# Splitting the gate-chunk stores, spreading the first gathers and V-group loads, and moving one exponent by two tiles

## The reference

```python
def peer_ffn(h, w_q, keys, u_tab, v_tab):
    ...
    q = (ht @ w_q).reshape(t, PEER_HEADS, 2, PEER_HALF)
    sc = jnp.einsum('thid,hikd->thik', q, keys).astype(jnp.float32)
    top_s, top_i = lax.top_k(sc, PEER_TOPK)
    cand = top_s[:, :, 0, :, None] + top_s[:, :, 1, None, :]
    best_s, best_pos = lax.top_k(cand.reshape(t, PEER_HEADS, PEER_TOPK * PEER_TOPK), PEER_TOPK)
    i1 = jnp.take_along_axis(top_i[:, :, 0], best_pos // PEER_TOPK, axis=-1)
    i2 = jnp.take_along_axis(top_i[:, :, 1], best_pos % PEER_TOPK, axis=-1)
    experts = i1 * N_KEYS + i2
    gates = jax.nn.softmax(best_s, axis=-1).astype(h.dtype)
    ...
    def block(args):
        hb, eb, gb = args
        act = jnp.einsum('thkd,td->thk', u_tab[eb], hb)
        coef = gb * jax.nn.gelu(act, approximate=False)
        return jnp.einsum('thk,thkd->td', coef, v_tab[eb])
```

## Time and profile before

| | |
|---|---|
| median of three runs | 3256.0 us |
| the profiled execution | 3247.32 us, its span 3245.6 us |
| TensorE busy, matmul | 3078.6 us (95% of the span) |
| VectorE, ScalarE, GpSimd busy | 75%, 47%, 26% |
| moved by DMA | 840.83 MB, mean 259 GB/s |
| U stage of the first layer | about 476 to 1118 us of the span |
| its V stage | about 1118 to 1663 us |

### The profile page before, as it was taken

The page is one execution under the profiler, slowest core; times in us unless marked ns, Lnnn a source line. Parts: engine busy times, 40 slices in busy tenths (PEclk is TensorE's granted clock), DMA queues, the critical chain, the costliest instruction groups (busy, mean ns, idle before and its releaser), DMA issues.

```text
span 3245.6 us, 47711 instructions
## 1 busy us (share of the span) xinstructions
PE 3078.6 (95%) x17460; PEld 2859.4 (88%) x17460; DVE 2436.0 (75%) x4276; ACT 1510.6 (47%) x2394; POOL 844.4 (26%) x655
## 2 busy tenths in 40 slices
PE   6988899999999999999989789999999999999998
PEld 3755679999999999999978468899999999999998
DVE  4564689778886688888876648995888857887887
ACT  3342223467886333333343522335878843333333
POOL 1000015544443222222200000354444422222221
PEclk8989999999999999999999889999999999999999
DMA  6524445589999999999932012467999999999996
GB/s 236 182 72 155 176 168 169 177 283 369 342 338 356 338 352 347 346 348 348 347 105 72 20 65 79 122 192 229 337 335 369 338 369 327 348 347 347 350 345 219
DMA packets 256496, 840.83 MB, mean 259 GB/s; under 512 B 23280, under 2 KB 72688, under 8 KB 248304
## 3 DMA queue, kind: packets, MB, share of 16 engines
q1 hardware_dynamic: 174000, 470.28, 41.8%
q0 software_dynamic: 80640, 318.80, 26.9%
q10 hardware_dynamic: 1728, 50.33, 3.7%
HBM read 736.56 MB, written 102.76 MB: 259 GB/s over the span
## 4 chain that ended last, share of the span: by engine, by line
PE 83%; DVE 7%; DMA 5%; ACT 4%; issue 1%; POOL 0%; DVEq 0%; SPq 0%; ACTq 0%; POOLq 0%
PE bank L815 41%; PE bank L1211 32%; PE bank L1195 4%; DMA w_raw<-wst 3%; PE bank L831 2%; PE bank L869 1%; ACT w_hi L571 1%; DMA activations<-act_out 1%; PE bank L1133 1%; DMA ada_buf<-adaw 1%; DVE w_lo L1253 1%; DMA ring<-u,gidx 0%; PE bank L964 0%; PE bank L981 0%; DVE zs L1533 0%
## 5 line engine op out<-in xcount | busy, mean ns | idle before, releaser
L571 ACT ACTIVATE w_hi<-w_raw 128x1024 fp32r<-128x1024 f32 x596 | 631.3, 1059 | 999.4 <-PE bank L815 759.8
L1253 DVE TENSOR_TENSOR w_lo<-w_raw,w_hi 128x1024 fp32r<-128x1024 f32 x516 | 632.2, 1225 | 610.2 <-ACT w_hi L571 609.3
L815 PE MATMUL bank<-hH,w_hi 128*128 128x384 f32 (+1 forms) x2656 | 948.1, 357 | 31.8 <-issue 7.9
L815 PE MATMUL bank<-hL,w_hi 128*128 128x384 f32 (+1 forms) x2656 | 928.5, 350 | 0.0
L815 PE MATMUL bank<-hH,w_lo 128*128 128x384 f32 (+1 forms) x2656 | 928.4, 350 | 0.0
L1211 PE MATMUL bank<-c_hi,w_hi 128*128 128x384 f32 x2048 | 686.1, 335 | 4.4 <-ACT act_out L747 3.2
L1211 PE MATMUL bank<-c_hi,w_lo 128*128 128x384 f32 x2048 | 684.3, 334 | 0.0
L1211 PE MATMUL bank<-c_lo,w_hi 128*128 128x384 f32 x2048 | 684.3, 334 | 0.0
L815 PEld LDWEIGHTS bank<-hH,w_hi 128*128 128x128 f32 x2656 | 504.1, 190 | 83.9 <-issue 42.5
L815 PEld LDWEIGHTS bank<-hH,w_lo 128*128 128x128 f32 x2656 | 503.2, 189 | 25.2
L815 PEld LDWEIGHTS bank<-hL,w_hi 128*128 128x128 f32 x2656 | 503.9, 190 | 22.1
(11 more groups left out here) (259 smaller groups left out, 2723.6 us busy)
## 6 DMA issues: line engine op xcount, KB each, us to landing
w_raw<-wst SPq DMA_DIRECT2D x596, 512.0 KB, 5.8
activations<-act_out SPq DMA_DIRECT2D x128, 384.0 KB, 6.5
gate_matrices<-stage ACTq DMA_DIRECT2D x12, 4096.0 KB, 17.1
act_in<-activations SPq DMA_DIRECT2D x64, 768.0 KB, 7.1
gates<-gate_matrices SPq DMA_DIRECT2D x64, 768.0 KB, 11.1
ada_buf<-adaw POOLq DMA_DIRECT2D x32, 1024.0 KB, 6.7
nrm<-adaw POOLq DMA_DIRECT2D x8, 1024.0 KB, 5.1
pj<-adaw POOLq DMA_DIRECT2D x4, 1024.0 KB, 5.5
```

The source lines that it names most:

```text
L571: nc.scalar.activation(w_hi[g % 2][:, :, :].rearrange("p a b -> p (a b)"), w_raw[:, g % RAWS, :], ACT.Copy).then_inc(s_wh, 1)
L815: last = mm(bank[s][:, 0:t.stop - t.start], a[s][:, k, :], b[:, k, t], start=(k == 0 and a is w_hi and b is hH), stop=(k == KT - 1 and a i ...
L1253: v.tensor_tensor(w_lo[g % 2][:, :, :].rearrange("p a b -> p (a b)"), w_raw[:, g % RAWS, :], w_hi[g % 2][:, :, :].rearrange("p a b -> p (a ...
```

## The change

It has four parts.
- The store of a gate chunk (4 MB, 32 KB in each partition) becomes four stores of 1 MB (8 KB in each partition, 32 keys each): one in the tile in which the chunk is full, and one in each of the three tiles after. The counts of the semaphores `s_gst` grow fourfold.
- `load_group` is cut in two, `load_acts` and `load_gates`. The first two groups are loaded ahead of the loads of tiles 116 (activations 0), 118 (gates 0), 120 (activations 1) and 122 (gates 1). The wait for all stores of the layer moves from 118 to 116. The later groups are loaded as before.
- The first five gathers are issued one behind each low part of tiles 20 to 24 instead of all behind that of tile 20.
- The first group's exponent is taken in tile 6 instead of tile 4; those of the other groups stay.

```diff
+STORES = 4
+STORE_KEYS = N_KEYS // STORES
+
+def stores_of(n):
+    return [(c, part) for c in range(GCHUNKS) for part in range(STORES)
+            if (c + 1) * CHUNK_QUADS - 1 in quads_of(n - part)]
...
-            def load_group(l, g):
+            def load_acts(l, g):
                 s = g % 2
...
                 sp.dma_start(act_in[s][:, :, :, :], a_dram[g * 2:g * 2 + 2].rearrange("q p b t -> p q b t")
                              ).then_inc(s_ain[s], 16)
+
+            def load_gates(l, g):
+
+                s = g % 2
                 sp.dma_start(gates[s][:, :, :, :],
...
+                    if n == U0 + GATE1 + 8:
+
+                        for s in range(2):
+                            sp.wait_ge(s_gst[s], (l + 1) * (GCHUNKS // 2) * STORES * 16)
+                        load_acts(l, 0)
                     if n == U0 + GATE1 + 10:
-
-                        for s in range(2):
-                            sp.wait_ge(s_gst[s], (l + 1) * (GCHUNKS // 2) * 16)
-                        load_group(l, 0)
-                    if n == U0 + GATE1 + 16:
-                        load_group(l, 1)
+                        load_gates(l, 0)
+                    if n == U0 + GATE1 + 12:
+                        load_acts(l, 1)
+                    if n == U0 + GATE1 + 14:
+                        load_gates(l, 1)
...
                         pool.wait_ge(s_gidx, l + 1)
-                        for k in range(RING):
-                            gather(l, k)
+                    if 0 <= n - (U0 + 2 * PICK_TILES) < RING:
+                        gather(l, n - (U0 + 2 * PICK_TILES))
...
-                    if tt < NT and m == 4:
+                    if tt < NT and m == (6 if tt == 0 else 4):
                         act.wait_ge(s_shift, l * NT + tt + 1)
...
-                        if i == CHUNK_QUADS - 1:
-
-                            act.wait_ge(s_gv, l * QUADS + q + 3)
-                            act.dma_start(g_dram[c].rearrange("p e t -> p (e t)"),
-                                          stage[c % 2][:, :, :].rearrange("p e t -> p (e t)")).then_inc(s_gst[c % 2], 16)
+                    for c, part in stores_of(n):
+                        e = slice(part * STORE_KEYS, (part + 1) * STORE_KEYS)
+                        act.wait_ge(s_gv, l * QUADS + (c + 1) * CHUNK_QUADS + 2)
+                        act.dma_start(g_dram[c][:, e, :].rearrange("p e t -> p (e t)"),
+                                      stage[c % 2][:, e, :].rearrange("p e t -> p (e t)")).then_inc(s_gst[c % 2], 16)
```

More of the change, by code:

```diff
@@ L91 @@
 assert [q for n in range(N_KEYS) for q in quads_of(n)] == list(range(QUADS))
+STORES = 4
[3 more added lines that the diff above has]
+            if (c + 1) * CHUNK_QUADS - 1 in quads_of(n - part)]
+assert sum(len(stores_of(n)) for n in range(N_KEYS)) == GCHUNKS * STORES
 RING = 5
@@ L464, in _ @@
                         sp.dma_start(keys[:, :, :], keysT[l]).then_inc(s_keys, 16)
+                    if n == U0 + GATE1 + 8:
+                        for s in range(2):
+                            sp.wait_ge(s_gst[s], (l + 1) * (GCHUNKS // 2) * STORES * 16)
+                        load_acts(l, 0)
                     if n == U0 + GATE1 + 10:
-                        for s in range(2):
-                            sp.wait_ge(s_gst[s], (l + 1) * (GCHUNKS // 2) * 16)
-                        load_group(l, 0)
-                    if n == U0 + GATE1 + 16:
-                        load_group(l, 1)
+                        load_gates(l, 0)
[3 more added lines that the diff above has]
+                        load_gates(l, 1)
                     if EV0 + 6 <= n < STREAM - 2 and (n - EV0 + 2) % GROUP == 0:
-                        load_group(l, (n - EV0 + 2) // GROUP)
+                        load_acts(l, (n - EV0 + 2) // GROUP)
+                        load_gates(l, (n - EV0 + 2) // GROUP)
                     load_w(l, n)
@@ L765, in _ @@
                         if i == 0 and l * GCHUNKS + c >= 2:
-                            act.wait_ge(s_gst[c % 2], (l * (GCHUNKS // 2) + c // 2) * 16)
+                            act.wait_ge(s_gst[c % 2], (l * (GCHUNKS // 2) + c // 2) * STORES * 16)
                         act.wait_ge(s_gm, l * QUADS + q + 1)
```

## The result

The changed kernel took 3203.9 us in the median of four runs (3202.3 to 3206.8), against 3253.9 of the kernel before: a ratio of 0.9841, 95% interval 0.9807 to 0.9874, 50 us or 1.6% faster. Forecast were 3223 us, 33 us faster, in a range from 3204 to 3243. The profiled execution took 3206.8 us with a span of 3205.0, against 3247.3 and 3245.6: 40.6 us less by the spans.

A forecast was written before the change was run, and what follows sets the result against it. Bound: TensorE matmul, 83% of the chain, with time to gain where it stands still or runs at lower clock. Terms -12.3 - 11 - 14 + 4 = -33.3 us took 3247.3 to 3214, plus 8.7 gave 3223; range 3204 to 3243.

The forecast's parts named there:

- Exponent, -12.3: First exponent, tile 4 of both layers: moved to tile 6, ScalarE no longer waits for VectorE's `bestv`; gain 12.3 us.
- Gathers, -11: First five gathers, GpSimd behind tile 20: spread one per tile, they no longer delay the low parts; gain 11 us.
- Middle stores, -14: Ten gate-chunk stores before each layer's last: 8 KB pieces let weight loads through; 17.1 us lost, 3 left, gain 14.
- parts that land in 5 to 8 us: Sign for the chunk stores: each 1 MB part lands 5 to 8 us after its issue.
- weight loads under 13 us: Sign for the chunk stores: weight loads take under 13 us.
- Last chunk and V groups, +4: SP's wait at tile 116 and packed V groups: 12 us lost in both layers against 7.9; cost 4 us.
- From the profile to the median, +8.7: Whole kernel: 8.7 us added to 3214, as the median shown stood that far above the profiled execution.
- (2): Chunk stores: stalls are a matter of bytes, not pieces, and stay; gain 19 us, time 3237; chance 0.17.
- (3): Tile 116: SP's wait and packed V groups cost 12 us a layer, not 6; time 3235 to 3243; chance 0.10.
- (4): All three stalls go, the last store's too: gain 48 us, time 3208; chance 0.17.
- (5): Spread gathers are late by 0.4 us in each tile: gain 29 us, time 3227; chance 0.03.
- (6): Chunk stores: four transfers hold the engines longer than one, up to 116 us for twelve, time 3349; chance 0.03.

The follow-up runs named there:

- before, again: The kernel before, unchanged, run and profiled once more: 3250.5 us in the median of eight.
- the part alone: The kernel before with only the first exponent moved from tile 4 to tile 6: 3242.7 us, ratio 0.9954.
- the split stores alone: The kernel before with only the chunk stores in four parts over four tiles: 3224.5 us, ratio 0.9910.

## Why the stores cost: the size of a piece, or how many at once

The changed kernel alters two things about a store, its pieces (8 KB for 32 KB) and its spreading over four tiles. Four kernels take them apart.

**All at once, in pieces of 8 KB.**

```diff
     return [(c, part) for c in range(GCHUNKS) for part in range(STORES)
-            if (c + 1) * CHUNK_QUADS - 1 in quads_of(n - part)]
+            if (c + 1) * CHUNK_QUADS - 1 in quads_of(n)]
```

> The changed kernel with all four parts of a chunk stored in the tile in which it is full: 4 MB at once, but in pieces of 8 KB. Theory A (turns piece by piece, size of the piece decides): a weight load beside them takes 7 to 12 us instead of 15, the four parts need about 20 us, middle stores lose 0 to 3 us in all, time within 5 us of the changed kernel. Theory B (spreading over four tiles is what helps): weight loads of 15 us and 17 us or more lost, 20 us slower than the changed kernel.

3237.2 us, ratio 0.9961 (0.9946 to 0.9975), and 38.9 us lost up to the copy behind tile 107, more than with one store of 4 MB. (4.2 of it belong to the last chunk's issues in tile 107 and are made up by the next copy, so 34.7 are the middle stores'.) The time, 33 us above the changed kernel, is nearer to theory B, but the reason is neither theory's. DMA issues, 717 to 734 us (KB each, us to landing), and the timeline of ScalarE there:

```profile
gate_matrices<-stage ACTq DMA_DIRECT2D x4, 1024.0 KB, 10.2
w_raw<-wst SPq DMA_DIRECT2D x2, 512.0 KB, 7.7
```

```profile
718.52 4.42 ACTq L796 DMA_DIRECT2D gate_matrices<-stage  x4
723.00 2.44 ACT L761 ACTIVATE oneh<-oneh,idxT 128x128 f32<-128x128 f32 x8 [4.50 <-issue]
725.35 1.04 ACT L592 ACTIVATE w_hi<-w_raw 128x1024 fp32r<-128x1024 f32 x1
```

The two weight loads of this stretch took 7.7 us, and with pieces of 32 KB it was 15.1; over both layers a load beside the parts took 8.9 us in the median. So shorter pieces do shorten the loads, and between 640 and 1010 us ScalarE waited for no transfer. But four issues in a row held ScalarE for 4.4 us here (2.7 to 4.9 us over the twelve chunks), where a single one takes 0.33, and the copy `w_hi` behind them came 3 us late or more: 9.3 us after the one before. With pieces of 8 KB it is this hold that spreading takes away.

**Two stores of 2 MB, pieces of 16 KB** (`STORES = 2`).

> The changed kernel with two stores of 2 MB over two tiles, pieces of 16 KB. By turns piece by piece a weight load takes 8 x (0.62 + 0.31) + 2.5 = 10 us, and up to 15 with the store of an activation pair ahead of it, against 14.1 + 1.9 us that it has. Theory A: 0 to 4 us lost at the ten middle stores. Theory B (bytes of one burst): half of the 17 to 26 us of before.

3209.2 us, ratio 0.9876 (0.9859 to 0.9892); 6.3 us lost at the middle stores, weight loads of 12.3 us where 10 was worked out. Between nothing at 8 KB and 17 to 26 at 32 KB. Theory A said 0 to 4 and theory B half of 17 to 26, so it is neither, nearer to A.

**Spread over four tiles, but in pieces of 32 KB, 32 neighbouring partitions each.**

```diff
-                        e = slice(part * STORE_KEYS, (part + 1) * STORE_KEYS)
+                        r = slice(part * (P // STORES), (part + 1) * (P // STORES))
...
-                        act.dma_start(g_dram[c][:, e, :].rearrange("p e t -> p (e t)"),
+                        act.dma_start(g_dram[c][r, :, :].rearrange("p e t -> p (e t)"),
```

> The changed kernel with a chunk's four parts cut by partitions instead of keys: four stores of 1 MB over four tiles, in pieces of 32 KB, two on each DMA engine. Theory A: two long rounds of 1.56 us and six short ones make a weight load of 5.0 us plus 2.5 to start, as with 8 KB; nothing lost. Theory B (pieces of 32 KB hold the weights up even in small numbers): 3 us or more lost at the middle stores.

3273.1 us, ratio 1.0061 (1.0042 to 1.0079), 70 us above the changed kernel, 59.5 us lost at the middle stores and 20 at the last. That looks like theory B, but it is one more effect. The page's queue row of the stores (packets, MB, share of 16 engines), first of this kernel, then of the next one:

```profile
q10 hardware_dynamic: 2304, 50.33, 5.1%
```

```profile
q10 hardware_dynamic: 2304, 50.33, 3.7%
```

The same bytes in the same number of packets held the engines for 5.1% of the span: 0.051 x 3273.6 x 16 / 1536 data pieces = 1.74 us for one, against 1.24 in the other.

**The same, but each part takes every fourth partition** (`r = slice(part, P, STORES)`).

> As the kernel whose parts were 32 neighbouring partitions, but each part takes every fourth partition, so that it reads from all over the buffer: four stores of 1 MB over four tiles in pieces of 32 KB. Theory A (the pieces of 32 KB were slow, 1.74 us against 1.24, because 32 neighbouring partitions share few ways out of the buffer): pieces of 1.2 us, 0 to 5 us lost at the ten middle stores, time within 8 us of the changed kernel. Theory B (long pieces hold the weights up even when few are under way): 20 us or more lost, weight loads of 12 us or more, as there.

3207.6 us, ratio 0.9857 (0.9828 to 0.9886), pieces of 1.24 us and 3.1 us lost at the middle stores. By pieces and time it is theory A. But weight loads still take 11.6 us beside such parts, where the sum of rounds in the expectation of the kernel ahead of this one gave 7.5. Which partitions a part reads costs 65 us.

**All of them together.** Where a trace has the landings, the weight loads of both layers that overlap a chunk store by over 3 us can be set beside what the middle stores lost:

| kernel | piece | stores of a chunk | load beside, median and longest | lost |
|---|---|---|---|---|
| neighbouring partitions | 32 KB | four, over four tiles | 15.0 and 19.8 us | 59.5 us |
| before, again | 32 KB | one | 13.6 and 16.4 us | 21.8 us |
| before | 32 KB | one | 13.3 and 16.1 us | 17.1 us |
| two stores | 16 KB | two, over two tiles | 12.3 and 15.5 us | 6.3 us |
| every fourth partition | 32 KB | four, over four tiles | 11.6 and 14.4 us | 3.1 us |
| changed, again | 8 KB | four, over four tiles | 10.5 and 13.9 us | 0.0 us |
| at once | 8 KB | four, in one tile | 8.9 and 10.8 us | 34.7 us, by the issues |

All but the last stand in one order: the longer the longest loads, the more is lost, and nothing is lost in the one kernel where the longest stays below the 14.1 us that the forecast gave a load from its issue to its use (in the gate tiles of the changed kernel 13.6 and 14.5 us lie between them in turn). Spreading alone brings most of that (3.1 us left), the shorter pieces the rest. Bytes are not out of it: by the forecast 477 GB/s are asked for over the four tiles and 421 can be moved, and that is the likely reason why a load in the changed kernel takes 10.5 us and not 7.5. It still comes in time, so this costs nothing.

That the engines take the queues in turn, piece by piece, can be seen in the kept trace of the kernel before. The 128 pieces of the second chunk's store, 1.21 us each, begin in eight groups of sixteen, about 1.5 us apart; in the middle of the store sixteen 4 KB pieces of SP's queue begin in each such group, as many as there are engines, and up to seventeen of the gathers. The eight pieces of an engine do not go in one run.

The Trainium skill, page SBUF — State Buffer, section Door 1: The DMA port swizzle, says that a partition's DMA port is given by bits 2 to 4 and bit 6 of its number: 32 neighbours reach 8 of the 16 ports, every fourth partition reaches all. By that rule the sixteen engines have half as many ports to read through in the one kernel as in the other. The trace agrees in direction, with 1.74 against 1.24 us, a factor of 1.4.

## The last chunk

**Wait and groups as before, rest changed.** `load_acts` and `load_gates` of group 0 ahead of 118, of group 1 ahead of 124, the wait at 118:

```diff
-                    if n == U0 + GATE1 + 8:
+                    if n == U0 + GATE1 + 10:
...
                         load_acts(l, 0)
-                    if n == U0 + GATE1 + 10:
                         load_gates(l, 0)
-                    if n == U0 + GATE1 + 12:
+                    if n == U0 + GATE1 + 16:
                         load_acts(l, 1)
-                    if n == U0 + GATE1 + 14:
                         load_gates(l, 1)
```

> The changed kernel with the first two V groups loaded as in the kernel before (both halves of group 0 ahead of tile 118, of group 1 ahead of 124, the wait for all stores at 118). Theory A (the earlier wait and the packed groups are what the last chunk still costs, 2.6 us in the first layer and 8.9 in the second): 5 to 10 us faster than the changed kernel, SP waits less than 3 us for the stores. Theory B (the bytes of these tiles decide, wherever the loads stand): within 2 us of the changed kernel.

3201.0 us (3200.0 to 3204.0), 5.3 us lost at the last chunks, SP waits at most 1.3 us for the stores. By the profiles 6 us better than the first of the changed kernel; by the medians 3, by the ratios (0.9837 against 0.9841) 1 us. The place behaves as theory A has it, the time does not reach its 5 us.

**Only the wait moved back to 116, groups at 118 and 124.**

> The changed kernel with the wait for all stores ahead of tile 116 as changed, but the V groups where they were (group 0 ahead of 118, group 1 ahead of 124). Theory A (the wait holds the weight loads back, which is what the last chunk costs): 4 to 8 us lost in the second layer behind the wait, SP stands 9 to 12 us before tile 116, time as the changed kernel. Theory B (the packed groups are what costs): 5 us lost in both layers together, as with the groups and the wait where they were.

3206.6 us, ratio 0.9856 (0.9828 to 0.9883). SP stood 8.7 us ahead of tile 116 in the second layer and yet only 2.5 us were lost there; 6.2 us in the first, with 3.9 lost, 6.5 together. That is 1.2 us more than without the wait. So a wait of 6 to 9 us in SP costs little by itself; the three tiles of weights ahead of TensorE are the likely reason, but that was not tried. Neither theory holds in full: more was lost than theory B's 5 us, and not where theory A put it.

**Groups at 118, 120, 122, 124, and at 119, 121, 123, 125.**

> The changed kernel with the wait and the first activations ahead of tile 118, the gates of group 0 ahead of 120, the activations of group 1 ahead of 122 and its gates ahead of 124. The stores have landed by then, so SP doesn't wait. Theory A (the wait is what costs): 3 to 6 us lost at the last chunks of both layers together against 11.5 in the changed kernel, 3197 to 3201 us. Theory B (bytes decide): no difference to the changed kernel.

> As the kernel with the groups from 118 on, one tile later again: ahead of 119, 121, 123 and 125, tiles that have no store of an activation pair behind them. Theory A: 1 to 5 us lost at the last chunks, 3196 to 3200 us, unless VectorE then waits for group 0 at its first product, which would cost up to 3 us a layer. Theory B (bytes decide): as the changed kernel.

3200.4 us (3198.8 to 3209.1) and 4.5 us lost; 3204.1 us (3200.0 to 3206.6) and 4.3 us lost; both have the ratio 0.9847, against 0.9841 of the changed kernel. VectorE waited for no group. The two differ by 4 us in the medians and by nothing at the place: that is the rest, 3194.4 against 3200.5, of which 4.3 us are the token mixer of the second layer and 2.4 its V stage. So theory A holds at the place in both, but a difference in time to the changed kernel isn't shown by these two.

**The three together on one chip.** Since the times above overlap, the changed kernel, the groups from 118 on, and the last chunk's four parts all in tile 107 were run side by side, five rounds each:

```diff
-            if (c + 1) * CHUNK_QUADS - 1 in quads_of(n - part)]
+            if (c + 1) * CHUNK_QUADS - 1 in quads_of(n - (0 if c == GCHUNKS - 1 else part))]
```

> The changed kernel once more, beside two variants on the same chip. Theory A (SP's wait ahead of tile 116 costs by itself): again 9 to 12 us of waiting in each layer and 8 to 12 us lost at the last chunks. Theory B (the 8.9 us of the first profile were a chance of the queues, the wait being absorbed by three tiles of weights in advance): 5 us or less. Middle stores 0.0 us in both.

> The groups from 118 on, once more (wait and first activations ahead of 118, then 120, 122, 124). Theory A: 3 to 6 us faster than the changed kernel on this chip, losses at the last chunks 4 to 5 us. Theory B: within 2 us of it.

> As the kernel before this, but the last chunk of a layer is stored in its own tile, four parts of 1 MB one behind the other, the other five spread over four tiles. Where all chunks went at once, the last ones lost only 1.0 us in both layers. Theory A (the last chunk's store should be through before the V groups come, and ScalarE has the time for four issues behind tile 107): 1 to 2 us lost at the last chunks, 2 to 4 us faster than the kernel before this. Theory B (ScalarE is held 4.4 us by four issues in a row and copies late, as in the middle): 5 us or more lost.

| kernel | median, range | ratio to before | last chunk | SP's wait, two layers |
|---|---|---|---|---|
| changed | 3203.6, 3199.6 to 3209.0 | 0.9847 | 7.3 us | 10.2 and 10.6 us |
| groups from 118 on | 3200.3, 3198.1 to 3202.4 | 0.9837 | 3.9 us | 1.6 and 2.4 us |
| last chunk at once | 3200.7, 3199.0 to 3203.2 | 0.9838 | 4.6 us | none |

The second profile of the changed kernel has 7.3 us where the first had 11.5, so part of the 8.9 of the second layer was chance. Theory A of the changed kernel's repeat asked for 8 to 12 us and theory B for 5 or less, so neither is met. With the groups from 118 on, 3.4 to 7 us less is lost at the place. In time, only this last comparison was made side by side, and it gives 3.3 us, 0.1%, with intervals of 0.17% either way; the earlier ratios to before (0.9837 and 0.9847 against 0.9841) give 1 us for and 2 against. So a gain of the later groups in the whole time is not shown. Storing the last chunk at once gains nothing further, nearer to theory B than to A, but not for theory B's reason: the issues held ScalarE for 3.4 and 4.3 us, the copy behind them came 1.0 and 2.2 us late, and the next copy made up all of it. The 4.6 us lie in the tiles behind, 109 to 114, where ScalarE waited for weight loads. The 1.0 us that the expectation took from the kernel with all chunks at once was a matter of booking: with tile 107 counted in, that kernel lost 5.2 us at its last chunks.

## Why the prediction was right or wrong

**Exponent, -12.3:** right to the tenth in both layers (0 left of 12.3), and the part alone gave 0.46%. What was said to be next, the exponent of tile 14, waited 1.25 us instead of 0.3, harmless for the reason given.

**Gathers, -11:** right; 11.4 came, all of it. The 0.5 us kept back for slow gathers were not needed: they took 0.95 to 1.00 us each, not the mean of 1.41, which is as short as before (0.93 us was the shortest). Why the mean is longer was not tried.

**Middle stores, -14: the term of the sum that was mis-sized.** In the mean 21.5 us were there to be had and all of it came. The mechanism held: the queues take turns by single pieces, as the starts of the pieces show, and a load that keeps within its 14.1 us costs nothing. Two sizes were off. The 17.1 us that I took as what is lost was the least of four profiles of kernels with big stores: 17.1, 20.7, 21.8, 26.2, mean 21.5. And I left 3 us, because more bytes are asked for in those four tiles than the engines move; 0.0 us were left in every kernel with 8 KB parts over four tiles. The surplus did show, but in the loads: beside parts they took 10.4 us in the median where 7.5 was forecast, 11.1 behind the store of an activation pair (forecast 12.2), 13.9 at most, and the parts landed after 6.3 to 11.7 us instead of 5. The sum for a load counts one transfer at a time in SP's queue; a load is issued every 5.5 us, so at 10.4 us two are under way at once. No run takes this apart further. Loads came in time as forecast, but with 0.2 us left of the 14.1 instead of 1.9, so that nothing at all was lost is partly luck. The two signs "parts that land in 5 to 8 us" and "weight loads under 13 us" were not fully met.

**Last chunk and V groups, +4:** right in kind, the one step that spoke against the change. SP's wait was forecast at 9 us and was 10.2 to 11.5; 12 us lost were forecast for both layers, 11.5 and 7.3 measured, against 7.9 and 9.0 before. It is +3.6 between the first profiles and +0.9 between the means, 9.4 after and 8.5 before.

**From the profile to the median, +8.7: the step that made the forecast wrong.** By the spans the forecast was -33.3 and -40.6 came, of which -37.2 is in the four places and -3.4 in the rest. The -3.4 is no gain of the change: the token mixer of the second layer was 4.9 us shorter at a higher granted clock (0.94 against 0.92), as it also was, by 7.4, in the second profile of before. To 3214 I then added the 8.7 us by which the median of three runs stood above the profiled execution of before, as if it belonged to the kernel. It does not: the second profile of before lies 3.5 us below the median of its runs, the one of the changed kernel 2.8 us above. And 3256.0, the median of three, was high: 49 runs of before, taken beside all the kernels here, have a median of 3252.4 and go from 3244 to 3268, the slower ones at a lower mean granted clock (3261 at 0.972, 3249 at 0.978). Without the 8.7 the forecast is 3214. With the sizes measured in the mean and the better start it is 3252.4 - 12.3 - 11.4 - 21.5 + 0.9 = 3208. The 4 us that remain are less than the rest varies between profiles of one kernel (7 us in the kernel before); what they are stays open.

**Rivals.** (2), bytes and not pieces, with the stalls staying, is out by the split stores alone. (3), 12 us a layer at the V groups, did not happen: 11.5 and 7.3 us for both layers together. (4), all stalls gone at 3208, was nearest in time, but by luck: the last chunk's stall stayed, and the middle ones gave more than the first profile showed. (5) did not happen. (6), four transfers hold the engines longer, is out: the stores' queue held the engines for 3.7% of the span before and after. But a form of it is real: a split by neighbouring partitions does so, 5.1%, and is slower than the kernel before.

## What to carry to other kernels

A large store holds up what is loaded beside it by the length of its pieces and by how many of them are under way at once: issue it in parts a tile apart, cut along the row inside each partition, not by neighbouring partitions, and not all parts in a row, because that holds the engine that issues them. What counts is the longest load beside it against the time that a load has. Ahead of a sum of stalls, read the same stalls in a second execution, since what a queue causes varies, and don't add the distance of one profiled execution to a median of three runs: it is scatter. Keep a wait for a store away from a queue of loads until the store has landed, but expect little from that where three tiles are loaded in advance, as here.

## What the runs showed of the hardware that I had not expected

- Four stores of 1 MB issued in a row by ScalarE held it for 2.7 to 4.9 us in twelve cases, one alone for 0.33 us.
- A piece of 32 KB took 1.74 us of an engine when the 32 pieces of a store came from neighbouring partitions, and 1.24 us when from every fourth. The kernels took 3273 and 3208 us.
- In each round of sixteen 32 KB pieces, about 1.5 us long, sixteen pieces of SP's queue began: the queues take turns by single pieces.
- Gathers on GpSimd took 0.95 to 1.0 us each in tiles 20 to 24, 1.38 us in the mean over all u gathers.
- The untouched parts differ by 12 us between seventeen profiles. Most of it is the token mixer of the second layer, 396.2 us at a granted clock of 0.95 and 403.6 at 0.92, and the V stage behind it with the end of the program, 556 to 562 us.
